# Squares of the later norms added in pairs on VectorE before the summing matmuls

## What is computed

```python
def rms_norm(x, g):
    xf = x.astype(jnp.float32)
    y = xf * lax.rsqrt(jnp.mean(xf * xf, axis=-1, keepdims=True) + EPS)
    return (y * g.astype(jnp.float32)).astype(x.dtype)

def hybrid_layer(x, ...):
    h = rms_norm(x, norm1)
    z = h @ w_in                       # (B, S, 5120), split among three mixers and their gates
    ...
    merged = gates[:, :, 0] * y_a + gates[:, :, 1] * y_b + gates[:, :, 2] * y_c
    x = x + merged @ w_out
    h = rms_norm(x, norm2)
    x = x + (jax.nn.silu(h @ w_gate) * (h @ w_up)) @ w_down
    return x
```

## Time and profile before

| | us |
|---|---|
| median of 3 runs (2078.09 to 2083.53) | 2078.76 |
| the profiled execution | 2079.5 |
| its span, slowest core | 2077.9 |
| spans of the 8 cores | 2069.8 to 2077.9 |
| busy: TensorE matmul | 1983.5 (95%) |
| busy: VectorE | 1005.4 (48%) |
| busy: ScalarE | 675.9 (33%) |
| mean granted TensorE clock of the 8 cores | 0.986 to 0.990 |

### The profile page before, as it was taken

The page is one execution under the profiler, slowest core; times in us unless marked ns, Lnnn a source line. Parts: engine busy times, 40 slices in busy tenths (PEclk is TensorE's granted clock), DMA queues, the critical chain, the costliest instruction groups (busy, mean ns, idle before and its releaser), DMA issues.

```text
span 2077.9 us, 31140 instructions; the slowest of 8 cores (2069.8 to 2077.9 us)
## 1 busy us (share of the span) xinstructions
PE 1983.5 (95%) x11536; PEld 919.7 (44%) x11536; DVE 1005.4 (48%) x1480; ACT 675.9 (33%) x1122; POOL 87.2 (4%) x164
## 2 busy tenths in 40 slices
PE   3799899999999999999999989999999999999996
PEld 1344544444444444444444454444444444444443
DVE  6789564444454444433353875544436223133135
ACT  6633682222333203115242258322224110111123
POOL 1001000000000000000000000000000000000000
PEclk9899999999999999999999999999999999999998
DMA  9537242112422313135378644212142220412103
GB/s 238 122 66 138 52 102 42 33 29 41 142 51 46 67 17 69 32 67 97 86 195 164 137 84 82 70 33 41 31 139 55 41 39 3 71 31 51 31 11 162
DMA packets 57235, 156.31 MB, mean 75 GB/s; under 512 B 6016, under 2 KB 26880, under 8 KB 54528
## 3 DMA queue, kind: packets, MB, share of 16 engines
q0 software_dynamic: 22032, 79.14, 22.8%
q1 hardware_dynamic: 32176, 72.03, 11.7%
q10 hardware_dynamic: 2880, 3.15, 0.6%
HBM read 193.58 MB, written 25.17 MB: 105 GB/s over the span
## 4 chain that ended last, share of the span: by engine, by line
PE 87%; ACT 4%; DVE 3%; issue 2%; DMA 2%; SPq 0%; DVEq 0%; ACTq 0%
PE ps L254 87%; DMA km<-k_mid 1%; DMA uc<-stg 1%; ACT yb L243 1%; ACT sq_s L243 1%; DVE cv L224 1%; ACT po L243 0%; DVE h L232 0%; SPq L270 0%; DVE gt L224 0%; ACT ph L243 0%; ACT L243 0%; ACT ps L243 0%; ACT g L243 0%; DVE idx L228 0%
## 5 line engine op out<-in xcount | busy, mean ns | idle before, releaser
L254 PE MATMUL ps<-h,slot 128*128 128x512 bf16 x5376 | 1203.9, 380 | 8.7 <-DVE h L232 6.6
L254 PEld LDWEIGHTS ps<-h,slot 128*128 128x128 bf16 x5376 | 525.4, 98 | 643.4 <-issue 19.1
L224 DVE TENSOR_TENSOR actb<-ps,sgf 128x512 bf16<-128x512 f32 x176 | 121.5, 691 | 419.5 <-PE ps L254 400.2
L254 PE MATMUL ps<-actb,slot 128*128 128x512 bf16 x1408 | 305.9, 379 | 0.0
L243 ACT ACTIVATE sgf<-ps 128x512 f32<-128x512 f32 x176 | 105.1, 597 | 595.2 <-PE ps L254 585.6
L232 DVE SCALAR_TENSOR_TENSOR acc<-gt,ps 128x512 f32<-128x512 f32 x180 | 123.4, 687 | 238.9 <-PE ps L254 236.7
L243 ACT ACTIVATE gt<-ps,hb 128x512 f32<-128x512 f32 x192 | 130.8, 686 | 331.4 <-PE ps L254 331.2
L254 PEld LDWEIGHTS ps<-actb,slot 128*128 128x128 bf16 x1408 | 137.6, 98 | 165.9 <-issue 0.2
L224 DVE TENSOR_TENSOR x<-ps,x 128x512 f32<-128x512 f32 x192 | 130.2, 689 | 134.6 <-PE ps L254 134.6
L261 POOL DMA_DIRECT2D slot<-wts x150 | 79.3, 532 | 1826.8 <-PE ps L254 1788.0
L254 PE MATMUL ps<-mg,slot 128*128 128x512 bf16 x512 | 114.9, 386 | 5.8 <-DVE mg L232 5.8
(11 more groups left out here) (130 smaller groups left out, 1197.7 us busy)
## 6 DMA issues: line engine op xcount, KB each, us to landing
slot<-wts POOLq DMA_DIRECT2D x150, 512.0 KB, 6.9
x<-xT SPq DMA_DIRECT2D x16, 512.0 KB, 18.1
x<-xT SPq DMA_DIRECT2D x4, 2048.0 KB, 16.0
x_mid<-x SPq DMA_DIRECT2D x4, 2048.0 KB, 8.9
x<-x_mid SPq DMA_DIRECT2D x4, 2048.0 KB, 18.0
outT<-x SPq DMA_DIRECT2D x4, 2048.0 KB, 6.4
uc<-stg SPq DMA_DIRECT2D x64, 64.0 KB, 6.6
hc<-stg SPq DMA_DIRECT2D x32, 128.0 KB, 2.9
```

Of the source, the lines that this page charges most:

```text
L224: return (eng or dve).put(lambda e: e.tensor_tensor(out=out, in0=a, in1=b, op=op), after)
L254: ins = e.matmul(out, lhsT=a, rhs=b, start=start and i == 0, stop=stop and i == n - 1, **kw)
```

## The change

The eight squares of a later ("rb") block norm are written in f32 into two buffers SQF, one for even and one for odd tiles. VectorE adds each pair into a bf16 tile, so that SQ["rb"] has four tiles and `norm_stat` issues four summing matmuls. The last of these (for every norm, also the first norms "s" with their eight) is put as an instruction of its own that alone waits for the last square or sum; the ones before it wait for the others. The norm of the preceding block is called at dp = 2 instead of dp = 1, in `w_out` and in the last `down`, and `norm2(ORD[3])` behind the second up tile instead of the first. An add is put into VectorE's queue in the tile after its second square. Everything else is as before.

```diff
-    SQ = {k: at("sq_" + k, [8, 512], BF16, o) for k, o in (("rb", o_rb), ("s", o_rc))}
+    SQ = {"s": at("sq_s", [8, 512], BF16, o_rc), "rb": at("sq_rb", [4, 512], BF16, o_rb + 4096)}
+    SQF = [at("sqf%d" % i, [512], F32, o_rb + 2048 * i) for i in range(2)]
...
+    pairs_due, pairs_even, sqf_free = [], [None], [None]
+
+    def norm_pair(b, kt, sqs, after=()):
+
+        t = actv(SQF[kt % 2][:, :], X[:, b, kt], AF.Square, [x_tok[b][kt], sqf_free[0], *after])
+        if kt % 2:
+            pairs_due.append((kt // 2, [pairs_even[0], t], sqs))
+        pairs_even[0] = t
+
+    def norm_add():
+        for j, ts_, sqs in pairs_due:
+            sqf_free[0] = tt(SQ["rb"][:, j], SQF[0][:, :], SQF[1][:, :], ALU.add, ts_ + [sq_free["rb"][j]])
+            sqs.append(sqf_free[0])
+        pairs_due.clear()
...
     def norm_stat(b, where, sqs, after=()):
         i = bank()
-        t = mm(ps[:, i], [(ONESB[:, :], SQ[where][:, kt]) for kt in range(KT)], sqs + [bank_free[i], t_onesb])
+        n = len(sqs) - 1
+        mm(ps[:, i], [(ONESB[:, :], SQ[where][:, kt]) for kt in range(n)], sqs[:n] + [bank_free[i], t_onesb], stop=False)
+        t = mm(ps[:, i], [(ONESB[:, :], SQ[where][:, n])], [sqs[n]], start=False)
...
         def w_out(b):
-            todo = []
             for dp in range(8):
...
-                todo.append(dp)
-                if dp == 1 and b != ORD[0]:
+                if dp == 2 and b != ORD[0]:
                     norm2(ORD[ORD.index(b) - 1])
-                if dp:
-                    sqs[b] += [norm_sq(b, d, "rb", S["rb_done"]) for d in todo]
-                    todo = []
+                norm_add()
+                norm_pair(b, dp, sqs[b], S["rb_done"])
...
         for b in ORD:
             w_out(b)
+        norm_add()
...
-                        if f == 0 and b == ORD[0]:
+                        if f == 0 and b == ORD[1]:
                             norm2(ORD[3])
...
         for b in range(NB):
-            todo = []
             for dp in range(8):
                 t = down(b, dp)
-                todo.append(dp)
-                if dp == 1 and b:
+                if dp == 2 and b:
                     next_norm(b - 1)
-                if dp:
-                    sqs[b] += [norm_sq(b, d, "rb", rb_after) for d in todo]
-                    todo = []
+                norm_add()
+                norm_pair(b, dp, sqs[b], rb_after)
+        norm_add()
```

## The result

| | before | after |
|---|---|---|
| median, us (20 executions each) | 2079.78 | 2076.20 |
| ratio, 95% interval | | 0.998 (0.9972 to 0.9988) |
| both kernels timed again, beside the first experiments | 2082.04 | 2077.43 |
| ratio, 95% interval | | 0.9981 (0.9971 to 0.999) |
| the profiled execution; its span | 2079.5; 2077.9 | 2077.64; 2076.0 |

The account below looks back on a forecast made before the run. TensorE bound the kernel by a small margin, with VectorE and ScalarE together binding after the change; terms -1.5 - 2.0 - 1.15 - 2.0 + 1.9 = -4.8 us gave a median of 2074.0 us, range 2069.5 to 2079.

Parts of the forecast that it names:

- stalls 1.1 and 0.34: Stages of later norms: TensorE waits for the fourth pair add, 1.1 us first, then 0.34 us in the next round.
- a turn of 2.11: Behind the eight applies, one pair's add, residual add, square and handoffs take 2.11 us, ends 2.0 and 2.3.
- each w_out -2.0: w_out of both layers: 16 summing matmuls of 0.216 us fewer, less 1.44 us of stalls, 2.0 us gained each.
- the end +1.9: Last norm, without cover: TensorE waits 4.1 us for the third pair's add, and the stage loses 1.9 us.
- the bank wait of u_blk: After down of layer 0: u_blk's second tile waits for the PSUM bank of down's tile dp = 5, 0.85 us lost.
- The forecast of 1.15: Last down of layer 0: 2.0 us gained, 0.85 given back to the bank wait, so -1.15 us.
- The start was forecast at -1.5: First four norms: seven of eight summing matmuls no longer wait for the eighth square, 1.5 us gained, ends 0 and 2.
- the sentence on the tie: One pair of f32 buffers makes an even tile's square wait for the previous pair's add; VectorE and ScalarE step together.
- 1, VectorE keeps up: Pair steps hide; all 13.8 us of matmuls and the start's 1.5 are gained, 2063.5 us; chance 0.13.
- 2, the clock drops behind each stall: TensorE's clock falls after each 1.1 us stall, 5.4 us more in all, 2079.4 us; chance 0.08.
- 3, slow handoffs: VectorE-ScalarE handoffs inside a pair cost 0.36 us instead of 0.10, 14.0 us more, 2088.0 us; chance 0.05.
- 4, the strict VectorE: VectorE starts no operation until its pipe has emptied: 2.21 us a pair, sum +4.2, 2083 us; chance 0.02.

## Why the prediction was right

**The bound.** "VectorE and ScalarE together have become the bound": confirmed from both sides. Leaving the adds out gives 7.5 us more, doubling them costs 9.9 us in one stage.

**The sum.** -4.8 forecast, -4.2 and -4.0 measured. By its terms, from start to start as the prediction counted: stalls 1.1 and 0.34 against 1.09 and 0.39 here (2045.16 + 3 x 0.216 to 2046.21; 0.16 more than the idle times in all cases); a block of 15.03 against 15.07; a turn of 2.11 against 2.12; each w_out -2.0 against -1.96 on its shortest core; the end +1.9 against +1.98, with waits of 4.16 and 1.11 against 4.1 and 1.4; the bank wait of u_blk 0.85 against 0.86, an idle time of 0.70:

```profile
1070.32 5.34 PE L255 MATMUL ps<-h,slot 128*128 128x512 bf16 x24 [0.70 <-DVE x L225]
```

That wait is new (the earlier trace rows have none there). It lies behind the cut of down 0, where it takes back what the four matmuls fewer of the fourth norm give (4 x 0.216 = 0.86), so the gain stays at the stage's 0.75. The forecast of 1.15 was 0.4 too high for another reason: the two stalls of down 0 cost 1.45 and 0.39 instead of 1.1 and 0.34, and 2.59 - 1.84 = 0.75. The first is longer because the first turn behind the applies takes 2.48 there (adds at 1036.26 and 1038.74) and the next 2.11; what VectorE waits for in it isn't shown. The start was forecast at -1.5 and measured at -1.4 and -2.5, the latter outside the 0 to 2 given for it. The first and second sums, which wait for squares, moved as said. The timeline of the change:

```profile
22.61 3.20 PE L255 MATMUL ps<-sq_s,onesb 128*128 128x512 bf16 x8 [22.61 <-DVE bbar L225]
...
47.19 1.89 PE L255 MATMUL ps<-sq_s,onesb 128*128 128x512 bf16 x8 [0.56 <-ACT sq_s L244]
```

23.12 became 22.61, and the wait of 1.07 became 0.56: half a microsecond each. That the total came within 1 us is partly luck: the five stages add up to -5.3 us in the first trace of the change and to -2.9 in the second, and the time of the slowest core lies between. What is firm are the terms that repeat: the w_out stages on undisturbed cores, down 0 and the end.

**What was wrong inside it.** The step that failed is the sentence on the tie: "There is one pair of f32 buffers, so Square of an even tile waits for the add of the pair before", from which the two engines were said to step together. The trace shows that wait 60 times (130.4 us in all), but four buffers take it away and the turn stays at 2.12. The length of the turn had been worked out from the right pieces (add, residual adds, square, handoffs), which is why the number held; the cause is the order of VectorE's queue. A wait that is shown is not yet a wait that binds. A smaller slip: before the change VectorE was not within 4 us a block of being as full as TensorE but within 5 (20.81 against 31.00 us in two blocks).

**The rivals.** 1, VectorE keeps up: would have shown blocks 14.7 us apart; they are 15.07 apart. 2, the clock drops behind each stall: the window over the end of the 0.92 us stall has a granted clock of 1.00, and so have 40 us around each pair of stalls in w_out. 3, slow handoffs: residual add to square takes 0.10 (1997.73 + 0.69 to 1998.52), square to add 0.11 or less, add to matmul 0.15. 4, the strict VectorE: fell with the 2.12, since an add of 0.69 is followed by the next operation 0.60 after its start (2026.06 to 2026.67). The ends taken for a turn, 2.0 and 2.3, were wider than needed.

**The clock.** In both traces of the change no stretch at 0.50 follows the stalls of 0.23 to 1.29 us, on any core; after 4.16 us the window shows 0.50, and the last matmul is 0.58 us long against 0.38. The other runs show that the length of one gap does not decide alone. After 2.01 to 2.25 us the half clock came on seven cores of eight (above). The gap of 3.02 us (3.17 on core 0) in front of w_out in layer 0, the prediction's row for long gaps, is followed by it in the kernel before on cores 0, 1, 3 and 4 and not on the others: the 80 matmuls of 19.11 us in the earlier trace rows take 17.43 on core 2 (first line). And with the fourth norm where it was, the waits of 0.61 and 1.2 us, 2 us from start to start, are followed by a half-clock stretch at three of sixteen places (eight cores, two layers), here on core 2 in layer 1 (second line, a window):

```profile
536.14 17.43 PE L254 MATMUL ps<-mg,slot 128*128 128x512 bf16 x80 [3.02 <-DVE mg L232]
...
1599.00:1602.00 3.00, 3.00 (x9) 1.07 (x8) 0.69 (x1) 2.88 (x4) 0.00 (x0) 0.50 0.02 5
```

The Trainium skill, page TensorE: Matmul & The Clock Gate, section What's actually happening, has idleness as the cause of 1.2 GHz; the rows agree for the gap of 4.16 us, while after 2 to 3 us it comes on some cores and not on others. The change's stalls cost only themselves, but rival 2 was nearer than one row of a single core made it look.

## What to carry to other kernels

Price a moved instruction by its place in the queue, not by its engine's busy share: here VectorE was 48% busy, and an add of 0.69 us behind a burst of applies cost a turn of 2.12 us, while the same add in front of the burst cost nothing on the path. If an in-order engine both feeds another engine and takes its answer back, put the taking back as far behind the feeding as buffers allow, and in front of bursts. At the end of a kernel, where nothing covers a wait, keep the form with more matmuls and fewer handoffs. And where stages are compared between traces, take also the core on which the stage is shortest: it told the w_out stages apart to 0.02 us where medians moved by 0.96 without any change.

## What was not expected of the hardware

An intermediate granted clock of 0.81 while TensorE was full, in stretches of 3.9 to 7.7 us, stood on cores 4 to 7 of one chip in all four kernels traced there, with the adds or without them, and was not in any row of before beyond the two levels. The same gap of 3.02 us is followed by half clock on four cores and not on the other four. A half-clock stretch behind a gap of only 2.23 us made seven sums take 3.06 us where eight had taken 1.89. GpSimd's f32 add of 128 x 512 takes 1.27 us, 1.8 times VectorE's, and starts 0.14 us after ScalarE's square ends (2027.37 + 0.63 to 2028.14).
